# A hybrid attention and retention layer with experts: the heads of two retention outputs put between the first high products of the mixing

## The chip, the cores and the metric

The kernel runs on one core of one Trainium2 chip. The metric is the device time of one execution in microseconds (us); of the kernel before there are three runs, with a median of 1474.67 us. The engines are named as the profile names them: PE is the matmul engine (PEld its weight loads), DVE the vector engine, ACT the scalar engine, POOL the general one, SP the one that issues most DMAs. Each takes its instructions in order and waits at semaphores.

## The reference

What is computed is one decoder layer on 512 rows of 1024 numbers, cut here to what matters:

```
h    = rms_norm(x); proj = h @ w_in            # q, k, v of both groups, and a gate
d    = rms_norm(diff_attention(q, k, v))       # 4 heads of 128
r    = rms_norm(retention(rq, rk, rv)) * silu(rg)
       # per tile i of 128 rows and per head h:
       #   y = (q * decay) @ state[i-1]  +  (q k^T * decay mask) @ v
x    = x + concat(d, r) @ w_o                  # the mixing
h2   = rms_norm(x)
x    = x + moe(h2)                             # router, top 4 of 32 experts
out  = rms_norm(x)
```

## The kernel before

The 512 rows are four tiles of 128. Up to about 195 us of the span the kernel does the input projection and the attention; from about 278 us to the end it runs 33 passes, one or more for each expert. The change lies between these, in the stage of retention and mixing, which is written out by hand in one order for each engine, with counting semaphores between them. Each engine goes through its own list strictly in order.

**Retention output.** `ret_output(i)` makes the four heads of tile i's retention output on PE: for tiles 1 to 3 each head is one product of decayed queries with the state (L804) and one of masked scores with values (L806), both plain fp32, each of which the trace shows as two instructions. The outputs of tile 2 go to the PSUM tensor `pair[2]`, those of tile 3 to `pair[3]`. When the fourth head is done, `ret_out` is raised. ACT then sums the squares of the four heads (`ret_squares`, L1230) and takes a root (L1129); DVE takes reciprocals and multiplies output, norm and gate (`gate(i)`, L1621 and four L1625) and raises `ret_gated` and then `mix_ready`.

**Mixing.** Tile i of the mixed rows is transposed on PE (`mix_turn(i)`, eight transposes, L832) into two PSUM banks; ACT copies each bank rounded to fp32r (`mix_evict`, L1279, raises `mixT_by_act`); DVE subtracts that from the bank to get the low part (L1657, raises `mixT_by_dve`). PE then multiplies: `mix_high(i)` is 32 products of 512 columns, four for each k of 8 (L856 and L858, into `pair[1 + i % 2]`: `pair[1]` for tile 0, `pair[2]` for tile 1), and `mix_low(i)` 16 more (L871). In front of `mix_high`, `mix_turn` issues the retention output of the tile two further on, and waits:

```
                if i < 2:
                    ret_output(i + 2)
                    pe.wait_ge(ret_decayed, NT)
                    pe.wait_ge(ret_gated, 1 if i == 0 else 3)
```

The last wait is there since `mix_high(1)` overwrites `pair[2]`, in which tile 2's retention output stands until DVE's `gate(2)` has read it.

**Router.** `router(i)` transposes the new residual rows (eight, L889) into `pair[3]` and multiplies them by the router's weights (L898). `router(0)` waits for `ret_gated` of 4 (tile 3's retention output leaves `pair[3]`), for both halves of the first tile's residual sum (`x2_ready`, DVE L1721), and then for the copies of the transposes by ACT (L1297) and DVE (L1736).

The lists of the engines around the change, in their order:

```
PE : mix_turn(0) [with ret_output(2)], mix_high(0), mix_low(0),
     mix_turn(1) [with ret_output(3)], mix_high(1), router(0), mix_low(1), mix_turn(2), ...
ACT: ret_squares(1), mix_evict(0), ret_squares(2), mix_evict(1), ret_squares(3),
     x2_norm(0) (L1291 and a root), turned_by_act(0) (L1297), ...
DVE: mix_evict(0), gate(1), att_norm(2), att_norm(3), mix_evict(1), gate(2), gate(3),
     add_to_residual(0) (L1721), h2_scale(0) (L1725), h2_norm(0) (L1731),
     turned_by_dve(0) (L1736), choose(0) (L1742 and on), ...
```

Of the kernel before, what the change touches and what calls it, by code (L numbers as in the profile page):

```python
# [35 lines left out]
P = 128  # L36
# [10 lines left out]
CQ, CK, CV, CRQ, CRK, CRV, CRG = 0, 512, 1024, 1536, 1792, 2048, 2560  # L47
BLOCK_COLS = (CRG, CRQ, CQ, CK, CRV, CV)
NH = 4
# [71 lines left out]
def build(nc, x, positions, norm1_g, w_in, lambda_q1, lambda_k1, lambda_q2, lambda_k2, diff_norm_g,  # L121
# [3 lines left out]
    with ctx:  # L125
# [3 lines left out]
        def sem(name):  # L129
            return ctx.enter_context(nc.semaphore(name))  # L130
# [60 lines left out]
        def slot(n):  # L191

            return ring[:, n] if n < RAW else late_ring[:, n - RAW]

        def w(a, n, rows=P):
            return work[0:rows, a:a + n]


        proj = w(0, NT * PROJ).rearrange("p (i c) -> p i c", i=NT)
# [23 lines left out]
        st_s = w(18432, NT * 512).rearrange("p (i r a n) -> p i r a n", i=NT, r=2, a=2)  # L223
        state = slot(RAW + 1).rearrange("p k c -> p (k c)")[:, 0:3 * 2 * P].rearrange("p (j a n) -> p j a n", j=3, a=2)
        qdT = w(20480, 2 * SEQ).rearrange("p (a t) -> p a t", a=2)
# [88 lines left out]
        pair = [ctx.enter_context(nc.psum_tensor(f"pair{i}", [P, 2, 512], F32)) for i in range(4)]  # L314
# [68 lines left out]
        ret_out = sem("ret_out")  # L383
# [255 lines left out]
        def _(pe):  # L639
            ident = cst[:, C_IDENT:C_IDENT + P]  # L640
            pe.wait_ge(ident_loaded, 16)
            for i in range(NT):
# [8 lines left out]
                for k in range(KT):  # L651
                    if i == NT - 1 and k == KT - 1:
                        pe.wait_ge(cols_copied, 2)
                    mm = pe.transpose(bank[k][:, i * P:(i + 1) * P], resid[:, i, k * P:(k + 1) * P], ident)
# [3 lines left out]
            def of_tile(i):  # L658
                return slice(i * P, (i + 1) * P)
# [9 lines left out]
            for i in range(NT):  # L669
                for k in range(KH):  # L670
                    mm = pe.matmul(bank[i], hT_hi[:, k, of_tile(i)], w_lo[0][:, k, :], start=False, stop=False)
# [34 lines left out]
            for c in range(1, NCHUNK):  # L706
                b, a, s = c // 2, c % 2, c % PARTS
                pe.wait_ge(w_hi_made, c + 1)
                for i in range(NT):
                    if a == 0 and b >= 2:  # L710
                        pe.wait_ge(proj_by_act if i % 2 == 0 else proj_by_dve, 2 * (b - 2) + i // 2 + 1)
                    dst, at_i = bank[NT * (b % 2) + i], of_tile(i)
# [5 lines left out]
                    for k in range(KH):  # L718
                        mm = pe.matmul(dst, hT_hi[:, KH * a + k, at_i], w_lo[s][:, k, :],  # L719
                                       start=False, stop=(a == 1 and k == KH - 1))  # L720
# [50 lines left out]
            ret_scores_at, ret_out_at = (1, 2, 3, 1), (2, 3, 2, 3)  # L771
# [18 lines left out]
                                   qkT[rows, RQ_AT + h // 2, i * P:(i + 1) * P], start=True, stop=True)  # L790
                mm.then_inc(ret_scores, 1)

            def ret_output(i):
                pe.wait_ge(ret_decayed, (2, 3, 3, 4)[i])
                if i >= 1:
                    pe.wait_ge(state_ready, 2 * i)
                    pe.wait_ge(qd_ready, 2)
                if i >= 2:
                    pe.wait_ge(ret_gated, i - 1)
                for h in range(NH):  # L800
                    rows = slice(64 * (h % 2), 64 * (h % 2) + 64)
                    dst = pair[ret_out_at[i]][:, h % 2, (h // 2) * P:(h // 2 + 1) * P]
                    if i >= 1:
                        pe.matmul(dst, qdT[rows, h // 2, i * P:(i + 1) * P], state[rows, i - 1, h // 2, :],  # L804
                                  start=True, stop=False)
                    mm = pe.matmul(dst, st_s[:, i, h % 2, h // 2, :],  # L806
                                   proj[:, i, CRV + h * P:CRV + (h + 1) * P], start=(i == 0), stop=True)
                mm.then_inc(ret_out, 1)

            pe.wait_ge(exp_done, 2 * NU)  # L810
            pe.wait_ge(attT_ready, NU)
# [2 lines left out]
            for i in range(NT):  # L814
                ret_score(i)
            ret_output(0)
            ret_output(1)


            def mix_turn(i):  # L820
                pe.wait_ge(mix_ready, i + 1)
                if i == 0:
                    pe.wait_ge(state_ready, 2 * (NT - 1))
                else:
                    pe.wait_ge(mixT_by_act, 2 * i)
                    pe.wait_ge(mixT_by_dve, 2 * i)
                if i == NT - 1:
                    pe.wait_ge(bias_out_ready, 2)
                for k in range(KT):
                    if k == 4:  # L830
                        mm.then_inc(mix_transposed, 1)
                    mm = pe.transpose(bank[k // 4][:, (k % 4) * P:(k % 4 + 1) * P],  # L832
                                      mix[:, i, k * P:(k + 1) * P], ident)
                mm.then_inc(mix_transposed, 1)
                if i < 2:
                    ret_output(i + 2)
                    pe.wait_ge(ret_decayed, NT)
                    pe.wait_ge(ret_gated, 1 if i == 0 else 3)
                else:
                    pe.wait_ge(x2_ready, 2 * (i - 1))  # L840

            def mix_high(i):
                dst = pair[1 + i % 2]
                last = i == NT - 1
                for k in (reversed(range(KT)) if last else range(KT)):
                    q, n = divmod(k, 2)
                    if k % 4 == 0 and not last:
                        pe.wait_ge(mixT_by_act, 2 * i + k // 4 + 1)
                    if k == KT - 1 and last:
                        pe.wait_ge(mixT_by_act, 2 * i + 2)  # L850
                    if i == 0:
                        pe.wait_ge(wo_hi_made, k + 1)
                        pe.wait_ge(wo_lo_made, k + 1)
                    for f in range(2):
                        cols = slice(f * 512, (f + 1) * 512)
                        pe.matmul(dst[:, f, :], mixT_hi[:, i % 2, k, :], wo_hi[q][:, n, cols],  # L856
                                  start=(k == (KT - 1 if last else 0)), stop=False)
                        mm = pe.matmul(dst[:, f, :], mixT_hi[:, i % 2, k, :], wo_lo[q][:, n, cols], start=False, stop=False)  # L858
                    if last and n == 0:
                        mm.then_inc(w_out_used, 1)  # L860
# [61 lines left out]
            def bias_product(i):  # L922
# [6 lines left out]
                for f in range(2):  # L929
                    pe.matmul(pair[0][:, f, :], gateT[:, i * P:(i + 1) * P],  # L930
                              b_out_parts[:, f * 512:(f + 1) * 512], start=True, stop=True).then_inc(bias_out_product, 1)

            mix_turn(0)
            mix_high(0)
            mix_low(0)
            mix_turn(1)
            mix_high(1)
            router(0)
            mix_low(1)
            for i in range(2, NT):  # L940
                mix_turn(i)
                places(i - 2)
                mix_high(i)
                bias_product(i - 2)
                router(i - 1)
                mix_low(i)
# [17 lines left out]
            for j in range(NT):  # L964
                mm = pe.matmul(bank[3][:, 64:64 + NE], ones_bf[:, :], picked_bf[:, j, :],
                               start=(j == 0), stop=(j == NT - 1))
# [1189 lines left out]
```

## Time and profile before

| what | value |
|---|---|
| three runs | 1474.67 us median (1473.21 to 1475.01) |
| profiled execution | 1473.39 us, of which the span in the trace is 1471.7 us |
| busy share of the span | PE 98%, PEld 80%, DVE 87%, ACT 69%, POOL 16% |
| mean granted clock of PE | 0.998 of full speed |
| stage of retention outputs and mixing | about 196 to 278 us of the span |

Times in the rows below are us from the start of the span. In a timeline a row is one or more instructions of one line: start, length, engine, line, operation, output and inputs, count; in brackets stands how long the engine was idle before it, and what released it. Matmuls overlap, so that the length of one is longer than the distance to the next; distances of starts are what a matmul costs.

### The profile page before, as it was taken

To read this page: it belongs to the slowest core of one execution; us is meant where nothing else is said; L and a number is where in the kernel's file an instruction comes from. 1 tells how busy PE (TensorE), PEld (TensorE's weight loads), DVE (VectorE), ACT (ScalarE), POOL (GpSimd) and SP (SyncE) were. 2 spreads that over 40 slices of the span, in tenths; PEclk is the share of its full clock that TensorE was granted. 3 is DMA by queue.
4 is the path that set the end of the run, shared out by engine and by line. 5 is a ranking of instruction groups with operands and counts; after the bars stand their busy time and mean duration, and the time that the engine had idled before them with its cause. 6 is when DMAs were issued, how large, how long until landed. Compare 5 with 4: busy or idle time off the path is not lost.

```text
span 1471.7 us, 21956 instructions
## 1 busy us (share of the span) xinstructions
PE 1441.0 (98%) x6833; PEld 1183.4 (80%) x6833; DVE 1277.7 (87%) x1120; ACT 1019.0 (69%) x876; POOL 240.9 (16%) x232
## 2 busy tenths in 40 slices
PE   7999899999999999999999999999999999999997
PEld 6888578778888888888888888888888888888885
DVE  5465747799999999999999999999999999999998
ACT  5423734667777777777777777777777777777774
POOL 0100302412111111111111111212111111111111
PEclk9999999999999999999999999999999999999999
DMA  9442101899999999999999999999999999999994
GB/s 342 177 182 120 44 0 66 303 345 373 365 371 357 375 363 370 367 364 379 364 376 371 379 368 358 389 369 363 373 372 368 370 367 372 367 375 365 367 358 168
DMA packets 131391, 471.72 MB, mean 321 GB/s; under 512 B 15304, under 2 KB 15596, under 8 KB 131176
## 3 DMA queue, kind: packets, MB, share of 16 engines
q1 hardware_dynamic: 118160, 451.46, 81.7%
q0 software_dynamic: 13024, 19.88, 5.5%
q8 instruction: 14, 0.23, 0.1%
q10 hardware_dynamic: 184, 0.08, 0.0%
q14 instruction: 9, 0.07, 0.0%
HBM read 467.44 MB, written 32.51 MB: 340 GB/s over the span
## 4 chain that ended last, share of the span: by engine, by line
PE 91%; DVE 4%; issue 2%; ACT 2%; DMA 1%; DVEq 0%; ACTq 0%
PE pair L993 24%; PE pair L985 24%; PE pair L987 24%; PE pair L714 3%; PE pair L719 3%; PE pair L715 3%; PE pair L999 2%; PE pair L1011 2%; PE pair L975 2%; DVE split L1815 1%; PE pair L856 1%; PE pair L871 1%; PE pair L858 1%; DMA ring<-in_w_moe_in 1%; ACT split L1325 0%
## 5 line engine op out<-in xcount | busy, mean ns | idle before, releaser
L1815 DVE TENSOR_TENSOR split<-ring,split 128x2048 fp32r<-128x2048 f32 x396 | 891.8, 2288 | 71.4 <-ACT split L1325 71.2
L1325 ACT CAST split<-ring 128x2048 fp32r<-128x2048 f32 x396 | 760.0, 1920 | 193.1 <-PE pair L993 190.7
L985 PE MATMUL pair<-split,operands 128*128 128x512 f32 x1584 | 630.0, 398 | 1.0 <-DVE operands L1821 1.0
L987 PE MATMUL pair<-split,operands 128*128 128x512 f32 x1584 | 618.0, 390 | 0.0
L993 PE MATMUL pair<-split,operands 128*128 128x512 f32 x1584 | 424.8, 390 | 0.9 <-DVE split L1815 0.9
L993 PEld LDWEIGHTS pair<-split,operands 128*128 128x128 f32 x1584 | 297.1, 188 | 65.1 <-DVE split L1815 2.1
L985 PEld LDWEIGHTS pair<-split,operands 128*128 128x128 f32 x1584 | 297.7, 188 | 60.1 <-DVE operands L1821 1.4
L987 PEld LDWEIGHTS pair<-split,operands 128*128 128x128 f32 x1584 | 297.9, 188 | 58.5
L2094 POOL DMA_INDIRECT expert_sums<-work,list_cur x32 | 61.8, 1932 | 455.3 <-PE pair L993 423.8
L2087 POOL DMA_INDIRECT work<-h_rows,token_next x34 | 75.2, 2211 | 183.4 <-DMA token_next<-slot_lists 166.7
L1334 ACT CAST operands<-pair 128x512 fp32r<-128x512 f32 x66 | 38.8, 589 | 68.8 <-PE pair L993 39.9
L714 PE MATMUL pair<-split,operands 128*128 128x512 f32 x176 | 68.8, 391 | 0.0
L2081 POOL DMA_DIRECT2D list_cur<-slot_lists x33 | 19.4, 589 | 300.4 <-issue 300.4
L715 PE MATMUL pair<-split,operands 128*128 128x512 f32 x176 | 68.5, 389 | 0.0
L1348 ACT CAST operands<-pair 128x512 fp32r<-128x512 f32 x66 | 38.5, 583 | 26.8 <-PE pair L1011 26.8
L1146 ACT CAST split<-ring 128x2048 fp32r<-128x2048 f32 x12 | 22.9, 1916 | 43.0 <-PE pair L719 37.3
L1832 DVE SCALAR_TENSOR_TENSOR work<-work 128x512 f32<-128x512 f32 x66 | 45.7, 693 | 6.9
L1509 DVE TENSOR_SCALAR work<-pair,stat 128x512 f32<-128x512 f32 x12 | 9.0, 750 | 46.4 <-PE pair L719 46.4
L719 PE MATMUL pair<-split,operands 128*128 128x512 f32 x176 | 47.1, 389 | 0.0
L1821 DVE TENSOR_TENSOR operands<-pair,operands 128x512 fp32r<-128x512 f32 x66 | 45.0, 684 | 1.0 <-ACT operands L1334 1.0
L1837 DVE TENSOR_TENSOR operands<-pair,operands 128x512 fp32r<-128x512 f32 x66 | 45.4, 688 | 0.0
L1828 DVE TENSOR_SCALAR work<-pair 128x512 f32<-128x512 f32 x66 | 45.2, 686 | 0.0
(268 smaller groups left out, 1149.4 us busy)
## 6 DMA issues: line engine op xcount, KB each, us to landing
ring<-in_w_moe_in SPq DMA_DIRECT2D x264, 1024.0 KB, 9.1
ring<-in_w_moe_out SPq DMA_DIRECT2D x132, 1024.0 KB, 9.9
ring<-in_w_in SPq DMA_DIRECT2D x12, 1024.0 KB, 10.5
ring<-in_w_o SPq DMA_DIRECT2D x4, 1024.0 KB, 10.3
resid<-in_x SPq DMA_DIRECT2D x4, 512.0 KB, 5.2
expert_sums<-zero_rows SPq DMA_DIRECT2D x4, 512.0 KB, 11.9
h_rows<-work SPq DMA_DIRECT2D x4, 512.0 KB
work<-expert_sums SPq DMA_DIRECT2D x4, 512.0 KB, 5.2
```

Of the source, the lines that this page charges most:

```text
L714: pe.matmul(dst, hT_hi[:, KH * a + k, at_i], w_hi[s][:, k, :], start=(a == 0 and k == 0), stop=False)
L715: pe.matmul(dst, hT_lo[:, KH * a + k, at_i], w_hi[s][:, k, :], start=False, stop=False)
L719: mm = pe.matmul(dst, hT_hi[:, KH * a + k, at_i], w_lo[s][:, k, :], start=False, stop=(a == 1 and k == KH - 1))
L985: pe.matmul(dst[:, f, :], left_hi[:, k0 + k, :], hi[c.buffer][:, k, cols], start=(start and k == 0), stop=False)
L987: pe.matmul(dst[:, f, :], left_lo[:, k0 + k, :], hi[c.buffer][:, k, cols], start=False, stop=False)
L993: mm = pe.matmul(dst[:, f, :], left_hi[:, k0 + k, :], lo[c.buffer][:, k, cols], start=False, stop=(stop and k == 1))
L1325: act.copy(hi[c.buffer], raw[c.slot]).then_inc(hi_made, 1)
L1815: dve.tensor_tensor(lo[c.buffer], raw[c.slot], hi[c.buffer].bitcast(F32), ALU.subtract).then_inc(lo_made, 1)
L1832: dve.scalar_tensor_tensor(result, gate, ACT_LIMIT, line, ALU.min, ALU.mult).then_inc(act_ready, 1)
L1837: dve.tensor_tensor(actT_lo[:, tiles, :], bank[7].rearrange("p (k t) -> p k t", k=KH), actT_hi[:, tiles, :].bitcast(F32), ALU.subtract).th ...
L2087: pool.indirect_dma_start(out=x_rows, out_offset=None, in_=h2_dram, in_offset=bass.IndirectOffsetOnAxis(ap=token_next[:, n:n + 1], axis=0) ...
L2094: pool.indirect_dma_start(out=sums_dram, in_=y_rows, in_offset=None, out_offset=bass.IndirectOffsetOnAxis(ap=dest_cur, axis=0), bounds_che ...
```

## The change

The function `ret_output` is taken apart into its waits (`ret_ready`) and one head (`ret_head`). Tiles 0 and 1 are issued as before. For tiles 2 and 3, `mix_turn` issues the waits and head 0 alone; heads 1, 2 and 3 stand inside `mix_high`, in front of the products of k = 2, 4 and 6. The waits behind the retention output in `mix_turn` now stand behind head 0. No instruction is added or taken away, and nothing changes in the lists of the other engines.

```diff
-            def ret_output(i):
+            def ret_ready(i):
                 pe.wait_ge(ret_decayed, (2, 3, 3, 4)[i])
                 if i >= 1:
                     pe.wait_ge(state_ready, 2 * i)
                     pe.wait_ge(qd_ready, 2)
                 if i >= 2:
                     pe.wait_ge(ret_gated, i - 1)
+
+            def ret_head(i, h):
+                rows = slice(64 * (h % 2), 64 * (h % 2) + 64)
+                dst = pair[ret_out_at[i]][:, h % 2, (h // 2) * P:(h // 2 + 1) * P]
+                if i >= 1:
+                    pe.matmul(dst, qdT[rows, h // 2, i * P:(i + 1) * P], state[rows, i - 1, h // 2, :],
+                              start=True, stop=False)
+                mm = pe.matmul(dst, st_s[:, i, h % 2, h // 2, :],
+                               proj[:, i, CRV + h * P:CRV + (h + 1) * P], start=(i == 0), stop=True)
+                if h == NH - 1:
+                    mm.then_inc(ret_out, 1)
+
+            def ret_output(i):
+                ret_ready(i)
                 for h in range(NH):
...
+                    ret_head(i, h)
...
                 if i < 2:
-                    ret_output(i + 2)
+                    ret_ready(i + 2)
+                    ret_head(i + 2, 0)
                     pe.wait_ge(ret_decayed, NT)
                     pe.wait_ge(ret_gated, 1 if i == 0 else 3)
...
                 for k in (reversed(range(KT)) if last else range(KT)):
                     q, n = divmod(k, 2)
+                    if i < 2 and n == 0 and k > 0:
+                        ret_head(i + 2, k // 2)
                     if k % 4 == 0 and not last:
                         pe.wait_ge(mixT_by_act, 2 * i + k // 4 + 1)
```

The list of PE in the kernel before, between the transposes of tile 1 (L832) and the first high products of tile 1 (L856, L858); L804 and L806 are the heads of tile 3:

```order
L832 MATMUL pair0<-cst,work 128x128 x7
L804 MATMUL pair3<-late_ring,work 128x128 [waits qd_ready,ret_gated,state_ready,ret_decayed]
L806 MATMUL pair3<-work 128x128
L804 MATMUL pair3<-late_ring,work 128x128
L806 MATMUL pair3<-work 128x128
L804 MATMUL pair3<-late_ring,work 128x128
L806 MATMUL pair3<-work 128x128
L804 MATMUL pair3<-late_ring,work 128x128
L806 MATMUL pair3<-work 128x128
L856 MATMUL pair2<-ring_split,operands 128x512 [waits mixT_by_act,ret_gated,ret_decayed]
L858 MATMUL pair2<-ring_split,operands 128x512
```

The same place in the changed kernel, where the transposes are L839, a head is L805 and L807, and the high products are L866 and L868:

```order
L839 MATMUL pair0<-cst,work 128x128 x7
L805 MATMUL pair3<-late_ring,work 128x128 [waits qd_ready,ret_gated,state_ready,ret_decayed]
L807 MATMUL pair3<-work 128x128
L866 MATMUL pair2<-ring_split,operands 128x512 [waits mixT_by_act,ret_gated,ret_decayed]
L868 MATMUL pair2<-ring_split,operands 128x512
L866 MATMUL pair2<-ring_split,operands 128x512
L868 MATMUL pair2<-ring_split,operands 128x512
L866 MATMUL pair2<-ring_split,operands 128x512
L868 MATMUL pair2<-ring_split,operands 128x512
L866 MATMUL pair2<-ring_split,operands 128x512
L868 MATMUL pair2<-ring_split,operands 128x512
L805 MATMUL pair3<-late_ring,work 128x128
```

One head instead of four now stands in front of the wait for `ret_gated`, and the second head stands behind eight products.

The end of that stretch in the kernel before, from the last high products of tile 1 to the router of tile 0 (L889 transposes, L898 products):

```order
L856 MATMUL pair2<-split,operands 128x512
L858 MATMUL pair2<-ring_split,operands 128x512
L889 MATMUL pair3<-cst,resid 128x128 [waits x2_ready,ret_gated]
L889 MATMUL pair3<-cst,resid 128x128 x3
L889 MATMUL pair3<-cst,resid 128x128 [waits x2_ready]
L889 MATMUL pair3<-cst,resid 128x128 x3
L898 MATMUL pair3<-late_ring,work 128x32 [waits h2T_by_act,router_scaled]
```

And in the changed kernel, from the fourth head of tile 3 on (the transposes of the router are L899 there, its products L908):

```order
L805 MATMUL pair3<-late_ring,work 128x128
L807 MATMUL pair3<-work 128x128
L866 MATMUL pair2<-split,operands 128x512
L868 MATMUL pair2<-ring_split,operands 128x512
L866 MATMUL pair2<-split,operands 128x512
L868 MATMUL pair2<-ring_split,operands 128x512
L866 MATMUL pair2<-split,operands 128x512
L868 MATMUL pair2<-ring_split,operands 128x512
L866 MATMUL pair2<-split,operands 128x512
L868 MATMUL pair2<-ring_split,operands 128x512
L899 MATMUL pair3<-cst,resid 128x128 [waits x2_ready,ret_gated]
L899 MATMUL pair3<-cst,resid 128x128 x3
```

The last head of tile 3 now has eight products between it and the router's transposes, where it had all 32.

## Rows read from the trace of the kernel before

**Rows 1.** The page: busy time by engine, and the chain that ended last.

```profile
PE 1441.0 (98%) x6833; PEld 1183.4 (80%) x6833; DVE 1277.7 (87%) x1120; ACT 1019.0 (69%) x876; POOL 240.9 (16%) x232
...
PE 91%; DVE 4%; issue 2%; ACT 2%; DMA 1%; DVEq 0%; ACTq 0%
```

**Rows 2.** Busy time in two stretches: window, length, PE, PEld, DVE, ACT, POOL, clock.

```profile
204.00:219.00 15.00, 15.00 (x73) 12.05 (x72) 3.80 (x9) 2.38 (x12) 0.00 (x0) 1.00 0.00 0
...
340.00:700.00 360.00, 360.00 (x1667) 297.83 (x1665) 335.23 (x223) 273.65 (x193) 57.58 (x50) 1.00 1.00 369
```

**Rows 3.** Timeline of all engines around tile 0's transposes and first high product.

```profile
200.07 0.29 PEld L804 LDWEIGHTS pair<-late_ring,work 64*128 64x128 f32 x2 [0.17 <-issue]
200.07 0.49 PE L804 MATMUL pair<-late_ring,work 64*128 64x128 f32 x2
...
200.68 1.05 ACT L1279 CAST operands<-pair 128x512 fp32r<-128x512 f32 x2
...
201.28 1.29 DVE L1657 TENSOR_TENSOR operands<-pair,operands 128x512 fp32r<-128x512 f32 x2 [1.67 <-ACT operands L1279]
...
203.23 0.47 PE L856 MATMUL pair<-ring_split,operands 128*128 128x512 f32 x1
```

**Rows 4.** Timeline from tile 0's low products to tile 1's first high products.

```profile
210.61 1.98 PE L871 MATMUL pair<-ring_split,operands 128*128 128x512 f32 x8
...
214.24 1.04 PE L832 MATMUL pair<-cst,work 128*128 128x128 f32 x8
...
215.21 0.48 PE L804 MATMUL pair<-late_ring,work 64*128 64x128 f32 x2
215.50 1.29 DVE L1657 TENSOR_TENSOR operands<-pair,operands 128x512 fp32r<-128x512 f32 x2 [10.20 <-ACT operands L1279]
...
216.91 1.13 DVE L1625 SCALAR_TENSOR_TENSOR work<-pair,stat,work 128x128 f32<-128x128 f32 x4
...
218.13 0.49 PE L806 MATMUL pair<-work 128*128 128x128 f32 x2
218.37 0.48 PE L856 MATMUL pair<-ring_split,operands 128*128 128x512 f32 x1
218.69 0.39 PE L858 MATMUL pair<-ring_split,operands 128*128 128x512 f32 x1
```

**Rows 5.** Timeline of ACT and DVE behind tile 3's last head.

```profile
221.67 1.29 DVE L1721 TENSOR_TENSOR resid<-resid,pair 128x512 f32<-128x512 f32 x2 [0.17 <-DVE work L1625]
...
224.18 0.30 ACT L1129 ACTIVATE stat<-stat,eps_col 128x1 f32<-128x1 f32 x1
...
224.71 1.28 DVE L1731 SCALAR_TENSOR_TENSOR work<-resid,stat,late_ring 128x1024 f32<-128x1024 f32 x1
```

**Rows 6.** Timeline of the router of tile 0, and the next low product.

```profile
225.72 1.03 PE L889 MATMUL pair<-cst,resid 128*128 128x128 f32 x8
...
226.35 0.59 ACT L1297 COPY work<-pair 128x512 f32<-128x512 f32 x1 [1.88 <-PE pair L889]
226.79 0.69 DVE L1736 COPY work<-pair 128x512 f32<-128x512 f32 x1 [0.80 <-PE pair L889]
...
227.09 0.38 PE L898 MATMUL pair<-late_ring,work 128*128 128x32 f32 x2 [0.33 <-ACT work L1297]
...
228.86 0.71 PE L871 MATMUL pair<-ring_split,operands 128*128 128x512 f32 x2
```

**Rows 7.** Timeline of the last router, whose transposes waited for the residual sum.

```profile
265.34 1.29 DVE L1721 TENSOR_TENSOR resid<-resid,pair 128x512 f32<-128x512 f32 x2 [0.99 <-PE pair L871]
...
266.18 1.16 PE L889 MATMUL pair<-cst,resid 128*128 128x128 f32 x8 [0.86 <-DVE resid L1721]
```

**Rows 8.** A stretch with PE all but idle; an idle PE, and the clock after.

```profile
294.10:296.90 2.80, 0.07 (x2) 0.00 (x0) 2.52 (x7) 0.00 (x0) 0.77 (x1) 1.00 1.02 398
...
14.13 0.50 PE L666 MATMUL pair<-split,operands 128*128 128x512 f32 x1 [3.61 <-ACT split L1146]
...
16.00:17.00 1.00, 1.00 (x4) 0.80 (x3) 1.00 (x3) 1.00 (x2) 1.00 (x3) 0.50 1.05 385
```

More of the change, by code:

```diff
@@ L799, in ret_output @@
                     pe.wait_ge(ret_gated, i - 1)
-                for h in range(NH):
[L801 to L808, printed above, removed]
+            def ret_head(i, h):
[10 more added lines that the diff above has]
+                ret_ready(i)
+                for h in range(NH):
+                    ret_head(i, h)
             pe.wait_ge(exp_done, 2 * NU)
```

## Prediction

> **What bounds the kernel now.** I read the page first: PE is busy 98% of the span, and the chain that ended last runs through it for 91% [rows 1]. Then the stretches: in the expert passes PE is busy all the time, with DVE close behind (335 of 360 us) [rows 2]. The changed stage is no different: from 204 to 219 us PE has no idle time at all, while DVE is busy 3.8 of 15 us and ACT 2.4 [rows 2]. So here PE's own list sets the pace, and a wait of another engine costs nothing as long as PE doesn't meet it. What the reader should look for in the timelines is therefore how much PE work stands between the moment another engine may start something and the moment PE asks for it. Twice in this stage that work is the retention heads.
>
> **The work that moves.** A head costs PE two pairs of instructions. In tile 3 the first pair starts at 215.21 and the eighth at 218.13 [rows 4], so a pair is 2.92 / 7 = 0.417 us, a head 0.834, and the three that move 2.50 us a tile. A high product costs 0.227 us: mix_high(0) takes 7.38 us for 32 (203.23 to 210.61) [rows 3, 4], of which some 0.1 is its start. Are heads dearer or cheaper between products? From the last pair (218.13) to L858 (218.69) it is 0.56 us, where a pair and a product would make 0.417 + 0.227 = 0.64: leaving a head gives back 0.08 [rows 4]. Entering one costs about 0.09: eight transposes in 1.04 us, one of them 0.27 long, are 0.11 apart, so the next place after 214.24 is 215.12, and the head starts at 215.21 [rows 4]. Together that is nothing, and I take 0 for the six moved heads; the bounds are 6 x 0.09 = 0.5 us dearer (only the entry), and 6 x 0.18 = 1.1 us cheaper (a pair of two loads of some 0.15 us each with the weight load of the first hidden wholly). At the entry the row shows the load starting with its matmul, both at 200.07 [rows 3], thus not hidden.
> The Trainium skill (TensorE: Matmul & The Clock Gate, "Part 2: What happens when you issue a matmul") says that the engine may pull a weight load ahead of a matmul in flight, so that the next weights load behind the running product. By that rule alone the heads would get cheaper among 512-column products; the row at 200.07 speaks against it for a head's first load.
>
> **Tile 0: a wait for ACT's first cast.** Before, PE had all four heads to do while ACT made the cast; the first high product started at 203.23, the cast was done long before. ACT starts its two casts at 200.68, since it was busy with tile 1's squares, and DVE's subtraction, which waits for the first of them, starts at 201.28 [rows 3]. Head 0 starts at 200.07 and is over at 200.90. So PE waits 0.4 us, and the first product starts at 201.30, 1.93 earlier than before; the three heads come back inside. The low products start at 210.61 - 1.93 + 2.50 = 211.18: **+0.57 us**. Bounds: 0.3 and 0.6.
>
> **Tile 1, first wait: gate(2).** mix_high(1) writes `pair[2]` and must wait until DVE's gate(2) has read it. gate(2) stands in DVE's list behind the two subtractions of tile 1's transposes (215.50, 1.29 us), and its four products run from 216.91 to 218.04 [rows 4]. Before, the heads covered this: PE came to the wait at 218.37, a third of a microsecond late. gate(2) hangs on the transposes, not on the heads, so it only shifts by the 0.57: over at 218.61, seen by PE at 218.66 (I allow 0.05 for a semaphore). PE comes with one head done: transposes at 214.81, head at 215.78, over at 216.61. **It stands still for 2.05 us** and has 2.50 us of heads yet to do. Before, mix_high(1) ran from 218.37 to 225.72 [rows 4, 6], 7.35 us; now it runs from 218.66 to 218.66 + 7.35 + 2.50 = 228.51. That is +2.79 in all so far.
> Tile 2's heads are late too (their squares need the fourth head, which now ends near 209.5), but DVE stood idle for 10.2 us before 215.50 [rows 4], so this is free; it would cost if that room were under 5 us.
>
> **Tile 1, second wait: gate(3) and all behind it.** The last pair of tile 3's heads now stands behind 24 products and nearly three heads: 218.66 + 24 x 0.227 + 0.09 (first product) + 1.67 (heads 1, 2) + 0.09 + 0.42 = 226.38, where it was 218.13: 8.25 us later. Queued behind it are, on ACT, the squares, the root, the norm of tile 0's residual and its root (to 224.48), and then the copy of the router's transposes; on DVE, gate(3), the residual sum L1721 (221.67), h2_norm (224.71 to 225.99) and the other copy [rows 5]. Their lists hold nothing else in between, so the chain moves as it is by 8.25. Before, it had room: the sum was done at 222.9, PE's transposes came at 225.72 [rows 5, 6]. Now:
> - L1721 starts at 229.92. In the last router the transposes started 0.84 us behind L1721's start, and took 1.16 us [rows 7]. So here at 230.76, PE having come at 228.51: **2.25 us idle**. Transposes over at 231.9.
> - ACT's root ends at 224.48 + 8.25 = 232.73, the copy L1297 follows, and the router's products start 0.74 after the copy starts (226.35 to 227.09 [rows 6]): 233.5. Another **1.6 us idle**.
> - The second half of these products needs DVE's copy, which can only start when h2_norm is over, at 225.99 + 8.25 = 234.24, and takes 0.69 [rows 5, 6]: 235.0. The products take 1.77 us (227.09 to 228.86 [rows 6]), so the first half is done at 234.4: **0.6 us idle**, then 0.89 us of work, to 235.9.
> The low products of tile 1 thus start at 235.9 in place of 228.86 [rows 6]: **+7.1 us**. From there each wait hangs on PE's own work as before: the choice of experts on the router's products, the first expert's weights on the last high products of the mixing, the first rows on the last router. I find no clock in this stage that isn't moved along, and the expert passes keep PE busy all the time [rows 2], so the 7.1 go to the end whole.
>
> **Sum.** Tile 0 gives 0.57, tile 1's first wait 2.79 - 0.57 = 2.22. From the end of mix_high(1) to the low products it takes 235.9 - 228.5 = 7.4 us in place of 228.86 - 225.72 = 3.14, which is 4.26 more (the three waits make 4.45, less the 0.33 that stood there before, plus slower transposes). Together 7.05; I say 7.1. Against the profiled execution, 1473.39 us, that is 1480.5; the median of the three runs is 1.28 above that execution, so the median becomes 1481.8.
>
> **The rivals.**
> - *The clock falls too.* From 228.5 to 235.9 PE would have some 2.9 us of light work in 7.4. Against a fall: in 294.1 to 296.9 PE did next to nothing and the granted clock stayed at 1.00; for it: PE had stood idle for 3.61 us before 14.13, and at 16 us the clock was 0.50, which is 1.2 of 2.4 GHz [rows 8]. A product costs twice its 0.227 us then; seven or eight of them would be 1.6 us: 1483.4. 13%. The Trainium skill (TensorE: Matmul & The Clock Gate, "The HAM clock gate") says that inactivity brings the throttle back and activity releases it; the fall behind the 3.61 us agrees.
> - *Only the first wait counts.* If the time behind the router were given back, because something later is the true limit, +2.8 is left: 1477.5. Against it is that no later wait in the mixing is as long as 1 us on PE. 8%.
> - *No change: all is absorbed where the experts begin.* The place is the first expert's product, which waits for weights and rows. If the weights came by a clock of their own and were 7 us late already, a late PE would cost nothing; this decides only if the weight loads don't move with PE. They are issued after `w_out_used` and `wo_done`, which PE raises. 1474.7; 5%.
> - *Faster: the heads get cheap.* The 1.1 us of hidden weight loads without any wait of PE gives 1473.6, still no measurable gain; to be faster by 0.2% both waits for gates would have to vanish and the loads hide. It decides from the point where gate(2) is over before 216.6, which DVE's list, with the subtractions ahead, rules out by 2 us. 2%.
>
> **How the numbers follow.** My own case has 72%. A measurement of this kernel tells about 0.2%, or 3 us, from no change. My case and the clock's are slower (85%), and half of "only the first wait" (it lies at the bound): 90% slower, 8% same, 2% faster. The range goes from 1479.0 (the heads at their cheaper bound, the waits somewhat shorter since an engine behind a wait picks up early, and the runs' own scatter of 1.5 us) to 1484.6 (the clock's case with the dearer heads).
>
> **What would show it.** In the changed kernel's trace: L866 of tile 0 starting at 201.3 behind a short idle time released by ACT's L1279; about 2 us idle in front of tile 1's first L866, released by DVE's gate products; in front of the router's transposes L899 2.2 us, released by the residual sum on DVE, and then waits in front of and amid L908, released by ACT's and DVE's copies; low products of tile 1 starting near 236. Outside this stage the distances are those of before. I would be wrong if PE reached the experts less than 7 us late, if heads between products cost other than 0.83 us, or if the granted clock left 1.00 near 236 us.

## The result, and the profile after

The changed kernel is slower: 1487.83 us median of 6 runs (1486.23 to 1488.91), against 1475.13 us (1473.21 to 1479.13, 6 runs) before; the ratio is 1.008, with a 95% interval of 1.0066 to 1.0094. That is 12.7 us, where I had forecast 7.1 and a range up to +10. The sign was right; the size was not.

The page after, with busy times, the granted clock in 40 slices, and the chain that ended last:

```profile
PE 1450.0 (98%) x6833; PEld 1189.2 (80%) x6833; DVE 1277.4 (86%) x1120; ACT 1018.8 (69%) x876; POOL 238.5 (16%) x232
...
PEclk9999998999999999999999999999999999999999
...
PE 91%; DVE 4%; issue 2%; ACT 2%; DMA 1%; SPq 0%; DVEq 0%; ACTq 0%
```

DVE, ACT and the chain are those of [rows 1], but for a few tenths of a us. But PE is busy 9 us longer with the same 6833 instructions (7.5 longer than in e11, a second profile of the kernel before, 1442.5 us), and the seventh slice of the clock row has an 8. Work that takes longer though nothing was added is a hint of the clock; idle time of PE would not make its busy time grow.

The timeline of PE after, which answers to [rows 3, 4, 6] (L839 transposes, L805 and L807 a head, L866 a high product, L899 and L908 the router, L881 low products):

```profile
200.39 1.04 PE L839 MATMUL pair<-cst,work 128*128 128x128 f32 x8
...
202.74 0.47 PE L866 MATMUL pair<-ring_split,operands 128*128 128x512 f32 x1 [0.48 <-issue]
...
212.68 1.98 PE L881 MATMUL pair<-ring_split,operands 128*128 128x512 f32 x8
...
216.31 1.03 PE L839 MATMUL pair<-cst,work 128*128 128x128 f32 x8
...
220.20 0.47 PE L866 MATMUL pair<-ring_split,operands 128*128 128x512 f32 x1 [2.02 <-issue]
...
229.51 0.49 PE L807 MATMUL pair<-work 128*128 128x128 f32 x2
...
233.89 1.16 PE L899 MATMUL pair<-cst,resid 128*128 128x128 f32 x8 [2.06 <-DVE resid L1731]
236.47 3.60 PE L908 MATMUL pair<-late_ring,work 128*128 128x32 f32 x16 [1.42 <-ACT work L1307]
239.88 3.76 PE L881 MATMUL pair<-ring_split,operands 128*128 128x512 f32 x8
243.44 2.87 PE L881 MATMUL pair<-split,operands 128*128 128x512 f32 x8
246.15 1.03 PE L839 MATMUL pair<-cst,work 128*128 128x128 f32 x8
```

This execution came to the mixing 1.3 us later than that of [rows 3] (its clock stayed low longer at the very start of the kernel), so distances are what counts. All the waits stand where the prediction put them: 0.48 us in front of tile 0's first product, 2.02 in front of tile 1's, 2.06 in front of the router's transposes, released by DVE's residual sum, and 1.42 in front of its products, released by ACT. A wait "<-issue" is one that the profile can't put down; what released it is seen on DVE:

```profile
217.57 1.29 DVE L1667 TENSOR_TENSOR operands<-pair,operands 128x512 fp32r<-128x512 f32 x2 [10.98 <-ACT operands L1289]
...
218.98 1.13 DVE L1635 SCALAR_TENSOR_TENSOR work<-pair,stat,work 128x128 f32<-128x128 f32 x4
...
231.76 1.13 DVE L1635 SCALAR_TENSOR_TENSOR work<-pair,stat,work 128x128 f32<-128x128 f32 x4
233.06 1.28 DVE L1731 TENSOR_TENSOR resid<-resid,pair 128x512 f32<-128x512 f32 x2 [0.17 <-DVE work L1635]
```

gate(2) runs to 218.98 + 1.13 = 220.11, and PE goes on at 220.20. What the prediction did not have in its sum is in the lengths: the router's 16 product records take 3.60 us (1.94 in the profile before; 0.3 of the difference is the wait amid them, which e2 shows below), and the 16 low products start over 239.88 to 246.15, 6.27 us, where before they took 228.86 to 232.63, 3.77. The stretches say why (columns as in [rows 2]):

```profile
218.00:220.00 2.00, 0.18 (x2) 0.00 (x0) 1.97 (x7) 0.02 (x1) 0.00 (x0) 1.00 0.00 0
...
222.00:224.00 2.00, 2.00 (x7) 1.12 (x6) 0.00 (x0) 0.00 (x0) 0.00 (x0) 0.50 0.00 0
...
228.00:230.00 2.00, 2.00 (x11) 1.39 (x10) 0.00 (x0) 0.00 (x0) 0.00 (x0) 1.00 0.00 0
...
232.00:234.00 2.00, 0.11 (x1) 0.14 (x2) 1.82 (x6) 0.00 (x0) 1.06 (x10) 1.00 0.00 0
...
236.00:238.00 2.00, 1.53 (x8) 1.56 (x8) 1.94 (x3) 1.61 (x2) 0.00 (x0) 0.50 0.03 8
...
242.00:244.00 2.00, 2.00 (x6) 1.52 (x6) 1.80 (x9) 0.14 (x1) 0.00 (x0) 0.50 0.00 0
```

The granted clock falls to half (1.2 of 2.4 GHz) twice in this stage: from 221.4 to 224.8, behind the 2 us of idle time, and from 235.1 to 245.3, behind the first of the router's waits and through the second. (This profile has two more falls, outside the stage: 13.4 to 20.2 us, and 293.0 to 296.6.) With PE busy throughout, six or seven records fit in 2 us at 0.50, and eleven at 1.00.

I measure the stage by the distance from the start of tile 0's transposes to that of tile 2's. Before it is 33.53 us (199.10 to 232.63), after 45.76 us (200.39 to 246.15): **+12.23 us**, nearly all of the 12.7 in the median. Behind it the kernel before and the changed one go alike (15.98 and 15.99 us to tile 3's transposes).

### The profile page after: what moved, and what is told of

Read it like the earlier page. It is cut to its first block, busy times and chain, and to the rows that moved or that the text cites. A ratio compares the mean times of both kernels' runs of the same rounds, so it can differ in the third digit from the quotient of the medians.

```text
span 1486.3 us, 21956 instructions
## 1 busy us (share of the span) xinstructions
PE 1450.0 (98%) x6833; PEld 1189.2 (80%) x6833; DVE 1277.4 (86%) x1120; ACT 1018.8 (69%) x876; POOL 238.5 (16%) x232
## 4 chain that ended last, share of the span: by engine, by line
PE 91%; DVE 4%; issue 2%; ACT 2%; DMA 1%; SPq 0%; DVEq 0%; ACTq 0%
PE pair L995 24%; PE pair L1003 23%; PE pair L997 23%; PE pair L714 3%; PE pair L715 3%; PE pair L719 3%; PE pair L1009 2%; PE pair L1021 2%; PE pair L985 2%; PE pair L881 1%; DVE split L1825 1%; PE pair L866 1%; PE pair L868 1%; DMA ring<-in_w_moe_in 1%; PE pair L908 1%
```

## The experiments

Each kernel was timed beside the kernel before on the same chip. "Stage" is the distance just defined, from one profiled execution of each kernel; the medians scatter by some microseconds even for one kernel, and the stage does not, so the stage carries the verdicts.

| kernel | stage us | over before | falls of the clock in the stage | ratio (95%) |
|---|---|---|---|---|
| before | 33.53 | | none | |
| e11, before again | 33.53 | 0.00 | none | 1.0001 (0.9989 to 1.0013) |
| changed | 45.76 | 12.23 | two | 1.008 (1.0066 to 1.0094) |
| e10, changed again | 45.74 | 12.21 | two | 1.0071 (1.0056 to 1.0086) |
| e1, tile 0 alone | 34.35 | 0.82 | none | 1.0007 (0.9994 to 1.002) |
| e2, tile 1 alone | 42.76 | 9.23 | second | 1.0074 (1.0054 to 1.0094) |
| e3, changed, spare work in both | 40.76 | 7.23 | none | 1.0048 (1.003 to 1.0066) |
| e4, first wait alone | 37.20 | 3.67 | first | 1.0028 (1.001 to 1.0046) |
| e5, changed, spare work in first wait | 43.30 | 9.77 | second | 1.0073 (1.0046 to 1.0101) |
| e6, changed, spare work at the router | 42.29 | 8.76 | first | 1.0054 (1.0033 to 1.0075) |
| e7, second wait alone | 40.53 | 7.00 | second | 1.0043 (1.0024 to 1.0061) |
| e9, changed, gate(2) early | 42.07 | 8.54 | second | 1.0051 (1.0037 to 1.0066) |

### Which tile's heads cost

**e1**, in which only tile 2's heads are put between products, against the changed kernel:

```diff
-                    ret_head(i + 2, 0)
+                    for h in range(1 if i == 0 else NH):
+                        ret_head(i + 2, h)
...
-                    if i < 2 and n == 0 and k > 0:
+                    if i == 0 and n == 0 and k > 0:
```

> Only tile 2's heads (those inside tile 0's mixing) are put between the products; tile 3's four heads stand in front of the high products of tile 1, as before. Theory A (waits of PE, and a granted clock that falls because PE stands idle or does little): 0.8 us over before (0.4 us of idle time for ACT's first cast and its ends), clock 1.00 throughout the mixing. Rival B (small heads among 512-column products cost by themselves, or lower the clock): half of the 12.7 us, some +6 us, with a clock under 1.00 in tile 0's mixing.

Measured: 1476.73 us against 1475.63 (23 runs of the kernel before), which can't be told from no change; the stage is 0.82 over. PE in e1:

```profile
198.89 1.04 PE L839 MATMUL pair<-cst,work 128*128 128x128 f32 x8
201.24 0.47 PE L867 MATMUL pair<-ring_split,operands 128*128 128x512 f32 x1 [0.48 <-issue]
...
214.85 1.04 PE L839 MATMUL pair<-cst,work 128*128 128x128 f32 x8
227.73 1.94 PE L909 MATMUL pair<-late_ring,work 128*128 128x32 f32 x16 [0.33 <-ACT work L1308]
233.24 1.04 PE L839 MATMUL pair<-cst,work 128*128 128x128 f32 x8
```

The fall of the clock that B asked for isn't there: in e1 the clock stays at 1.00 through the mixing. The whole 0.8 us lies in tile 0's part (15.96 us between its transposes and tile 1's, where the kernel before takes 15.14), 0.48 of it as the wait; the rest of the stage is as before. Heads among products thus neither lower the clock nor cost much: rival B falls.

**e2**, in which only tile 3's heads are put between products (the two edits of e1 with the tiles exchanged):

> Only tile 3's heads (those inside tile 1's mixing) are put between the products. Theory A: nearly the whole loss, +11 to +12 us: 2.05 us idle for gate(2), then the chain behind gate(3), and the clock at half speed behind each. Rival B: +6 us.

Measured: 1487.9 us, the whole loss within its interval. PE in e2:

```profile
200.72 1.04 PE L839 MATMUL pair<-cst,work 128*128 128x128 f32 x8
...
219.73 0.47 PE L867 MATMUL pair<-ring_split,operands 128*128 128x512 f32 x1 [2.02 <-issue]
...
231.91 1.16 PE L900 MATMUL pair<-cst,resid 128*128 128x128 f32 x8 [2.05 <-DVE resid L1732]
234.49 1.25 PE L909 MATMUL pair<-late_ring,work 128*128 128x32 f32 x8 [1.42 <-ACT work L1308]
236.04 1.92 PE L909 MATMUL pair<-late_ring,work 128*128 128x32 f32 x8 [0.30 <-DVE work L1747]
...
243.48 1.03 PE L839 MATMUL pair<-cst,work 128*128 128x128 f32 x8
```

All four waits are those of the changed kernel, and here the last one, for DVE's copy (0.30), shows as a row of its own. In this execution no fall came behind the first wait, so the stage is 9.23 over and not 11 to 12; a fall from 279.6 to 286.4 us and one from 310.3 to 313.7 brought the whole to the same time (behind tile 2's transposes e2 took 1243.1 us, the kernel before 1239.1).

### Keeping PE at work in the waits

**e3** is the changed kernel with spare matmuls where PE stands idle. Its additions:

```diff
+                    if i == 1:
+                        for n in range(2):
+                            ret_head(i + 2, 0)
                     pe.wait_ge(ret_decayed, NT)
...
+            def fill(n):
+                for m in range(n):
+                    pe.matmul(pair[0][:, m % 2, :], mixT_hi[:, 1, m % KT, :], wo_hi[0][:, 0, 0:512],
+                              start=True, stop=True)
...
+                    pe.wait_ge(mixT_by_dve, 4)
+                    fill(9)
                     pe.wait_ge(ret_gated, NT)
```

and in `router(0)` six more in front of the products and two amid them. Nothing of the result changes.

> The changed kernel, with spare matmuls of PE where it stands idle: head 0 of tile 3 made twice more in front of the wait for gate(2) (the same result), and 9, 6 and 2 products of 512 columns into pair[0], which the next transposes overwrite, ahead of the router's transposes, its products and their second half. Theory A with the clock as cause of what the waits don't explain: the waits stay, the clock stays at 1.00 to the end of the mixing, and about 4 to 5 us come back: +7.5 us over before (range 6.5 to 9), though PE has more to do. If the excess over my 7.1 us comes from the interleaving itself (B), nothing comes back, and some of the 19 spare instructions' time adds: +12.7 or more.

Measured: 1482.75 us. PE in e3, where L892 is the spare work:

```profile
198.85 1.04 PE L839 MATMUL pair<-cst,work 128*128 128x128 f32 x8
...
218.66 0.47 PE L869 MATMUL pair<-ring_split,operands 128*128 128x512 f32 x1 [0.35 <-issue]
...
228.59 2.20 PE L892 MATMUL pair<-ring_split,operands 128*128 128x512 f32 x9
230.80 1.16 PE L909 MATMUL pair<-cst,resid 128*128 128x128 f32 x8
...
235.85 2.10 PE L884 MATMUL pair<-ring_split,operands 128*128 128x512 f32 x8
237.78 1.99 PE L884 MATMUL pair<-split,operands 128*128 128x512 f32 x8
239.61 1.03 PE L839 MATMUL pair<-cst,work 128*128 128x128 f32 x8
```

This is the kernel of my sum, since its clock stays at 1.00 through the stage: the low products start 37.00 us behind tile 0's transposes (I had 235.9 - 199.10 = 36.8), and the stage is 7.23 over where I had worked out 7.05. With more work to do, PE is 5.0 us faster through the stage than in the changed kernel. The spare work itself delayed nothing: tile 1's first high product stands 19.81 us behind tile 0's transposes in e3 (198.85 to 218.66) and in the changed kernel (200.39 to 220.20), and from there the router's transposes come after 12.14 us in e3 and after 12.18 in e2 (219.73 to 231.91), which has no spare work and no fall there. So the excess is the clock's.

**e5** has only the first of e3's additions:

> The changed kernel with spare work in the first wait alone (head 0 of tile 3 made twice more). Theory A: the first fall of the clock, at 221 to 225 us in the changed kernel's trace, is gone (about 1.7 us of the way from tile 0's to tile 2's transposes); the second, behind the router's waits, stays. From tile 0's to tile 2's transposes 44 us, where the changed kernel took 45.8, the kernel before 33.5 and the one with all spare work 40.8. Rival C (a fall is a matter of chance, not of idle time): no different from the changed kernel.

**e6** has only those around the router:

> The changed kernel with the 17 spare products around the router alone. Theory A: the second fall of the clock (235 to 245 us in the changed kernel's trace) is gone, 3.3 us back; the first wait stays and may or may not be followed by a fall: from tile 0's to tile 2's transposes 40.8 us without, 42.5 with one. The median some 8 to 10 us over before. Rival C: no different from the changed kernel.

Measured: e5 1488.17 us, stage 43.30; e6 1484.51 us, stage 42.29. In e5 the first fall is gone and the second there; in e6 the other way round. First PE in e5 (the low products, at half clock, take 3.64 us), then in e6:

```profile
220.31 0.47 PE L869 MATMUL pair<-ring_split,operands 128*128 128x512 f32 x1 [0.35 <-issue]
...
238.45 3.64 PE L884 MATMUL pair<-ring_split,operands 128*128 128x512 f32 x8
```

```profile
216.97 1.03 PE L839 MATMUL pair<-cst,work 128*128 128x128 f32 x8
...
220.86 0.47 PE L866 MATMUL pair<-ring_split,operands 128*128 128x512 f32 x1 [2.02 <-issue]
...
223.33 0.79 PE L805 MATMUL pair<-late_ring,work 64*128 64x128 f32 x2
224.06 0.79 PE L807 MATMUL pair<-work 128*128 128x128 f32 x2
...
232.34 2.21 PE L889 MATMUL pair<-ring_split,operands 128*128 128x512 f32 x9
```

In e6 the head behind the first wait takes 0.79 in place of 0.48 a pair: the clock is low. Taking e3 from e6 gives the price of the first fall: 42.29 - 40.76 = 1.53 us. Another pair gives the same: from tile 1's first high product to the router's transposes the changed kernel takes 13.69 us, e2, without this fall, 12.18. Taking e3 from e5 gives a second fall of 2.54 us (235.0 to 242.0); for the changed kernel, where it lasted until 245.3, 45.76 - 40.76 - 1.53 = 3.47 us are left over. One profile of each kernel could not rule out rival C, that falls are chance; the count over all profiles (last section) speaks against it, though not wholly.

### One wait at a time

**e4** keeps the first wait but not the late gate(3):

```diff
                     pe.wait_ge(ret_gated, 1 if i == 0 else 3)
+                    for h in range(NH if i == 0 else 1, NH):
+                        ret_head(i + 2, h)
```

with tile 0 as before and no heads in `mix_high`.

> Tile 2's heads as before. Of tile 3, head 0 in front of the wait for gate(2), heads 1 to 3 right behind it, then the 32 high products in one piece. The first wait is kept (2.05 us idle), the lateness of gate(3) shrinks from 8.25 to about 2.2 us, which the 2.8 us of room before the router cover. Theory A: +2.2 us from the wait, and 1.5 to 2 more if the clock falls behind the 2 us of idle time: +2.2 to +4.2, no idle time before the router's transposes. Rival B: 0 to +1, since no head stands among products.

Measured: 1479.15 us; stage 3.67 over, with one fall. The row of the wait, and the router, in e4:

```profile
218.42 0.46 PE L805 MATMUL pair<-late_ring,work 64*128 64x128 f32 x2 [2.06 <-DVE work L1636]
...
231.06 1.94 PE L909 MATMUL pair<-late_ring,work 128*128 128x32 f32 x16 [0.33 <-ACT work L1308]
```

2.06 us of idle time, here put down to gate(2)'s line on DVE, and only 0.33 at the router, which also stood there before [rows 6]. 3.67 is 2.1 of waiting and about 1.5 of the clock, with no head among the products.

**e7** keeps heads 0 to 2 in front of the first wait and puts head 3 in front of k = 6:

> Tile 2's heads as before; of tile 3, heads 0, 1 and 2 in front of the wait for gate(2), head 3 in front of the products of k = 6. The first wait shrinks to 0.4 us, the lateness of gate(3) is 6.0 us in place of 8.25. Theory A: 2.2 us idle before the router's transposes (the products end 2.25 earlier too), the low products of tile 1 start 4.8 us late, and the clock falls behind that as in the changed kernel: 3 us more, +7.5 to +8.5 in all. A theory in which the first wait is the whole loss would give +0.8.

Measured: 1482.9 us; stage 7.00 over with a fall from 230.7 to 237.5, the first wait 0.35, those at the router 2.05 and 1.42. I had 4.8 for the waits and 3 for the fall; if the 4.8 holds, the fall gave about 2.2.

**e9** is the changed kernel with one exchange in DVE's list:

```diff
-            mix_evict(1)
             gate(2)
+            mix_evict(1)
             gate(3)
```

> The changed kernel with gate(2) ahead of tile 1's subtractions in DVE's list. DVE stands idle for 10 us there, and tile 2's heads are done by then. Theory A: the 2.0 us of idle time in front of tile 1's first high product are gone, and with them a fall of the clock behind it. Tile 3's fourth head is still 6.2 us late, so the waits around the router stay (2.3, 1.4 and 0.3 to 0.6 us) with a fall behind them: from tile 0's to tile 2's transposes +5.0 us without a fall and about +7.5 with one (38.5 to 41 us). If the first wait had hung on something else than the place of gate(2), it would stay.

Measured: 1484.74 us; stage 42.07, which is 8.54 over and 1.1 above the top of what I expected; the second fall lasted from 231.9 to 242.2, where in e5 and e7 it had lasted some 7 us. DVE in e9:

```profile
213.09 1.13 DVE L1635 SCALAR_TENSOR_TENSOR work<-pair,stat,work 128x128 f32<-128x128 f32 x4
217.90 1.29 DVE L1667 TENSOR_TENSOR operands<-pair,operands 128x512 fp32r<-128x512 f32 x2 [3.69 <-ACT operands L1289]
```

PE in e9, from tile 1's transposes to the router:

```profile
216.65 1.04 PE L839 MATMUL pair<-cst,work 128*128 128x128 f32 x8
230.41 1.16 PE L899 MATMUL pair<-cst,resid 128*128 128x128 f32 x8 [2.05 <-DVE resid L1731]
232.99 3.60 PE L908 MATMUL pair<-late_ring,work 128*128 128x32 f32 x16 [1.42 <-ACT work L1307]
```

gate(2) now runs at 213, ahead of the transposes, and between them (216.65) and the router PE has no idle time at all. The first wait was the place of gate(2) in DVE's list and nothing else.

### How steady it is, and an attempt at a gain

**e10**, the changed kernel again, and **e11**, the kernel before again:

> The changed kernel once more, for a second profile. Theory A: the waits are those of the first profile within 0.1 us (2.0, 2.1, 1.4); a fall behind the router's waits again; a fall behind the first wait perhaps (it came in the changed kernel, in e4 and in e6, not in e2). From tile 0's to tile 2's transposes 42.8 to 45.8 us.

> The kernel before once more, for a second profile. Theory A: no idle time over 0.4 us on PE in the mixing and 33.5 us from tile 0's to tile 2's transposes within 0.1; no fall of the clock there.

Measured: e10 1486.73 us, waits 2.02, 2.05 and 1.42, both falls, stage 45.74; e11 1477.43 us, no fall, stage 33.53. The stage repeats to 0.02 us; the medians do not (e10 is 9.5 us over the 1477.22 of the kernel before beside it, where the first measurement gave 12.7).

**e8** gives the kernel before spare work in two idle places:

```diff
+            def keep_warm(dst, n):
+                for _ in range(n):
+                    pe.matmul(dst, ident, resid[:, 0, 0:512], start=True, stop=True)
+
+            pe.wait_ge(hT_hi_made, 1)
+            pe.wait_ge(hT_lo_made, 1)
+            keep_warm(bank[0], 3)
             pe.wait_ge(w_hi_made, 1)
...
             list_passes()
+            keep_warm(bank[7], 3)
             act_transposes(0, 0)
```

> The kernel before, with 3 spare fp32 products of 512 columns (identity times a residual tile) in two places where PE stands idle: at 11 to 14 us, in front of the first product of the input projection (into a bank that is overwritten), and at 294 to 297 us, in front of the first pass's second transposes. Theory A: the fall of the clock at 15 to 19 us is gone and 1.4 us with it, and falls at the start of the experts become rarer: -1.5 to -3 us in the median. If idle time isn't what lowers the clock: 0 to +0.5.

Measured: 1477.2 us against 1475.68, ratio 1.001 (0.9994 to 1.0026): no gain, and the 1.5 to 3 us that I had expected did not come. By the median alone this is nearer to what I had set down for "idle time isn't what lowers the clock". Three stretches of e8:

```profile
14.00:19.00 5.00, 5.00 (x22) 3.78 (x21) 4.00 (x5) 4.97 (x9) 2.83 (x5) 1.00 1.06 370
200.00:206.00 6.00, 6.00 (x19) 4.30 (x18) 3.61 (x9) 0.94 (x6) 0.00 (x0) 0.50 0.01 3
272.00:275.00 3.00, 3.00 (x16) 3.00 (x16) 2.72 (x12) 1.28 (x3) 1.39 (x2) 0.50 1.03 415
```

The fall at the start, which all twelve other profiles have, is gone, and tile 0's transposes start at 197.60 us, 1.5 earlier than before. But two others came, from 196.6 to 207.0 and from 271.8 to 275.4 us, where none of the other twelve profiles had one; with the first of them tile 0's to tile 2's transposes took 37.71 us in place of 33.53. PE's waits before it are those of the kernel before (1.08 us before 194.00, there 1.07 before 195.86). With this, the spare work did nothing for the kernel as a whole. Why the falls came there was not found out, and idle time of PE need not be the only thing that decides on a fall.

## Why the prediction was right in kind and wrong in size

- **The heads' own cost: right.** I had 0.834 us each and nothing for entering and leaving, so 7.38 + 2.50 = 9.88 us for tile 0's 32 high products and three heads; in the changed kernel they take 9.94 (202.74 to 212.68).
- **Tile 0, +0.57: measured 0.82** (e1; 0.78 in the changed kernel). The first high product starts 2.35 us behind the transposes where I had 2.20, and the pieces among products cost 0.06 more.
- **First wait, 2.05: measured 2.02** (2.06 in e4), and gone when gate(2) is moved (e9).
- **The waits around the router, 2.25 + 1.6 + 0.6: measured 2.06 + 1.42 + 0.30** (changed, e2). The first is smaller in the rows, since the idle time that they show begins when the last matmul ends, while my sum counts from the place of the next start. The second is smaller because the products came 2.58 us behind the start of the transposes, where I had 2.74. The third was measured with the clock already low (in e2 from 235.0), so it doesn't test the 0.6.
- **Their sum, 7.05: measured 7.23** in e3, in which the clock doesn't fall.
- **The delay goes to the end whole: right.** From tile 2's transposes to the end of the span the five profiles without a fall at the start of the experts take the same within 0.6 us: before 1239.1, e11 1238.7, e3 1238.5, e4 1238.7, e7 1239.0. The eight with a fall there, or shortly before, take 1239.9 (e8) to 1244.6 (e1); the changed kernel's profile 1240.2. Such falls were seen in profiles with next to no loss in the mixing too (e1, e8), but in neither of the two profiles of the kernel before.
- **The step that failed is the clock.** The prediction took the clock at 1.00 for its sum and wrote a fall down as a rival with 13% and a price of 1.6 us, "seven or eight" products at twice 0.227. It speaks of one fall, at the router. There were two: 1.53 us behind the first wait, which I had not considered at all, and some 3.5 us at the router. The prediction had named a clock that leaves 1.00 near 236 us as a sign of being wrong; it left it at 235.1. The reason given against a fall, that the clock stayed at 1.00 through 2.8 us with PE all but idle [rows 8], is true and didn't carry: the first fall came behind an idle time of 2.0 us. The size of the rival was also too small: a product at the low clock did cost about twice (0.42 to 0.43 us from start to start behind 221.44), but the low clock lasted longer than "seven or eight" of them, to 245.3 us, 10.2 us in all, part of which the router's waits hid.

The Trainium skill (TensorE: Matmul & The Clock Gate, "HAM oscillation — how this bites in real kernels") describes the pattern: a kernel that works in short pieces with waits in between, and whose clock is back at half speed for each piece. The changed kernel's two falls, at two places with waits, agree with it in kind. In its example the waits are for DMA, each longer than the 2 us of work before it; here waits of 2.0 us amid far longer work, in front of tile 1's products or heads, were followed by a fall in four of five profiles.

## What to carry to other kernels

Before work of the busiest engine is moved out from in front of a wait, read what that work was hiding: here the heads hid the list of DVE up to gate(2), and their early end gave ACT and DVE the room for the router, 2.8 us, which a delay of 8 us overran. On PE, price an added wait with the clock in it: here 7.2 us of waiting cost 12.2. When a loss is larger than its waits, look whether the busy time has grown with the same instructions, and put harmless work in the wait to see which part is the clock's.

## What the runs showed of the hardware

- **Behind 2.0 us of idle time in the mixing the clock fell in most profiles.** Behind the 2.0 us in front of tile 1's products or heads the clock fell in four of five profiles (changed, e4, e6, e10) and not in e2, with the same instructions on both sides. With 0.5 us or less at this place it fell in none of the seven others, leaving e8 aside. At the unfilled waits of the router it fell in all six (changed, e2, e5, e7, e9, e10), and with the waits filled in neither of two (e3, e6).
- **The length of an idle time alone did not decide.** At the start of the experts PE stands idle for 2.76 or 2.77 us in every profile but e8 (before 296.93 in the kernel before). A fall began within 0.7 us of the end of that wait in four of the twelve (e2, e5, e6, e9), and in the other eight none did, the two of the kernel before among them. e8's falls at 196.6 and 271.8 us came behind waits of PE that stand in the kernel before too.
- **The time of one kernel scatters, and its clock with it.** In the runs of the kernel before beside e1 to e4 the mean granted clock goes from 0.998 (1472.7 to 1473.5 us) to 0.992 (1482.76 us). The fall at the start alone lasted from 15.3 to 18.7 us in one profile of the kernel before and from 13.4 to 20.2 in the other, and the second of these came to the mixing 1.6 us later (200.69 in place of 199.10). Not all of the scatter need be the clock's: in e1's profile PE waited 5.13 us before 308.23 for a DMA of gathered rows, in e5's 2.19 us before 317.15, and the other eleven profiles have no such wait.
- **The clock rose later than the work came back.** In the changed kernel PE had its low products without a break from 239.88 and the clock rose at 245.3; in e7 it had them from 234.63 and the clock rose at 237.5.
